# Expert layer on one core: the rows of each expert's list dealt round the partitions

## The reference, cut to what matters

```
g_sel = argmax(softmax(x @ w_rg)); top_p, top_i = top_k(softmax(le[g_sel]), 2)   # one of 4 groups, 2 of its 8 experts
gate  = p_sel * top_p / sum(top_p);  eid = g_sel * 8 + top_i
for each block of up to 128 rows of one expert e:
    y[rows] += gate * ((silu(x[rows] @ w_g[e]) * (x[rows] @ w_u[e])) @ w_d[e])
```

## Time and profile before

| what | value |
|---|---|
| median of 3 runs | 1541.19 us (1537.97 to 1541.45) |
| profiled execution | 1536.46 us, of which span 1535.0 us |
| TensorE busy | 1404.0 us, 91% of the span, mean granted clock 0.965 |
| VectorE, ScalarE, GpSimd busy | 1085.5, 859.4, 407.6 us |
| HBM read, written | 285.06 MB, 51.80 MB |
| weight loads | 96 x 2048 KB |
| gathers L2309, adding scatters L2318 | 32 and 30 |

### The profile page before, as it was taken

How to read it: one execution, slowest core, us unless ns; L and a number is a source line. 1 busy time by engine, 2 the same in 40 slices (tenths; PEclk the granted TensorE clock), 3 DMA queues, 4 the chain that set the end, 5 groups by cost and what they waited for, 6 DMA issues and landing times.

```text
span 1535.0 us, 23095 instructions
## 1 busy us (share of the span) xinstructions
PE 1404.0 (91%) x8472; PEld 1159.4 (76%) x8472; DVE 1085.5 (71%) x1526; ACT 859.4 (56%) x1029; POOL 407.6 (27%) x280
## 2 busy tenths in 40 slices
PE   5999899999978899986999959999999999999982
PEld 4788788888866777875888747888888777777771
DVE  4766765544456667663566768989998888888876
ACT  5644444433355555542444447777777777777764
POOL 2000111111132000000122243556654443444321
PEclk9999999999999999997999969999999999999996
DMA  8344412112311100013565558999999999999977
GB/s 272 118 152 145 161 66 103 68 65 83 103 42 49 58 25 28 15 49 116 171 247 211 197 196 305 390 392 393 387 392 385 378 367 375 370 379 381 380 270 292
DMA packets 63242, 329.12 MB, mean 214 GB/s; under 512 B 11862, under 2 KB 18406, under 8 KB 50882
## 3 DMA queue, kind: packets, MB, share of 16 engines
q1 hardware_dynamic: 45906, 278.60, 47.7%
q0 software_dynamic: 17264, 49.56, 10.6%
HBM read 285.06 MB, written 51.80 MB: 219 GB/s over the span
## 4 chain that ended last, share of the span: by engine, by line
PE 30%; DMA 13%; issue 4%; DVE 4%; ACT 2%; POOLq 0%; DVEq 0%; POOL 0%; SPq 0%; ACTq 0%
PE acc L96 9%; PE acc L98 9%; PE acc L97 9%; DMA plain<-in_w_gate 4%; DMA plain<-in_w_down 4%; DMA odd_gate<-in_w_gate 3%; ACT shared L1799 1%; PE acc L2414 1%; DVE even_lo L1804 1%; PE acc L2444 1%; PE acc L1994 1%; DVE plain L2617 1%; DMA s_x_mid<-plain 1%; DMA s_h_rows<-plain 1%; PE acc L2005 1%
## 5 line engine op out<-in xcount | busy, mean ns | idle before, releaser
L96 PE MATMUL acc<-shared,split 128*128 128x512 f32 x952 | 382.2, 401 | 16.8 <-DVE split L2062 11.4
L98 PE MATMUL acc<-shared,split 128*128 128x512 f32 x952 | 373.7, 393 | 0.0
L96 PEld LDWEIGHTS acc<-shared,split 128*128 128x128 f32 x952 | 180.9, 190 | 53.9 <-DVE split L2062 11.6
L1804 DVE TENSOR_TENSOR even_lo<-plain,shared 128x4096 fp32r<-128x4096 f32 x48 | 211.6, 4420 | 7.1 <-ACT shared L1799 6.3
L98 PEld LDWEIGHTS acc<-shared,split 128*128 128x128 f32 x952 | 180.3, 189 | 38.7
L96 PE MATMUL pa<-shared,a_xT_hi 128*128 128x512 f32 (+1 forms) x480 | 193.6, 403 | 16.2 <-DVE a_w_lo L736 14.0
L1799 ACT CAST shared<-plain 128x4096 fp32r<-128x4096 f32 x48 | 174.3, 3633 | 36.1 <-DMA plain<-in_w_up 14.5
L98 PE MATMUL pa<-shared,a_xT_lo 128*128 128x512 f32 (+1 forms) x480 | 187.0, 390 | 0.0
L97 PE MATMUL acc<-even_lo,split 128*128 128x512 f32 x384 | 150.6, 392 | 0.0
L1804 DVE TENSOR_TENSOR split<-odd_rest,shared 128x4096 fp32r<-128x4096 f32 x31 | 137.0, 4421 | 6.0 <-ACT shared L1799 5.8
L2309 POOL DMA_INDIRECT plain<-s_h_rows,plain x32 | 130.3, 4072 | 21.1 <-issue 11.8
(11 more groups left out here) (334 smaller groups left out, 2732.0 us busy)
## 6 DMA issues: line engine op xcount, KB each, us to landing
plain<-in_w_gate SPq DMA_DIRECT2D x16, 2048.0 KB, 19.6
plain<-in_w_up SPq DMA_DIRECT2D x16, 2048.0 KB, 20.4
plain<-in_w_down SPq DMA_DIRECT2D x16, 2048.0 KB, 20.3
odd_rest<-in_w_down SPq DMA_DIRECT2D x16, 2048.0 KB, 19.7
odd_gate<-in_w_gate SPq DMA_DIRECT2D x16, 2048.0 KB, 20.2
odd_rest<-in_w_up SPq DMA_DIRECT2D x16, 2048.0 KB, 21.3
a_x_turned<-in_x_turned SPq DMA_DIRECT2D x24, 512.0 KB, 3.5
a_x_row<-in_x SPq DMA_DIRECT2D x12, 512.0 KB, 4.9
```

Of the source, the lines that this page charges most:

```text
L96: pe.matmul(out, st_hi, mv_hi, start=first, stop=False)
L98: return pe.matmul(out, st_lo, mv_hi, start=False, stop=last)
L1804: eng.tensor_tensor(self.w_lo[half][m], self.raw[half][m][:, 0:4096], self.w_hi[m].bitcast(F32), ALU.subtract).then_inc(self.s_wlo[m], 1)
```

## The change

A helper `dealt` changes the order in which a table slice of 128 rows is read. The slice is seen as 8 groups of 16 rows and read with the 16 outermost: place 16h + l of a list goes to partition 8l + h, for h = 0 to 7 and l = 0 to 15. It is applied to each of the three fetches of lists. `places` gets the same order, so that the first expert's list, which does not come from the table, is dealt too. Rows, gates and table stay what they were; only the partition on which each row of a block stands is another, in the gather and in the adding scatter.

```diff
+ENGINES = 16
+
+def dealt(rows):
+    return rows.rearrange("(h l) c -> l h c", l=ENGINES)
...
-            nc.gpsimd.iota(places[:], pattern=[[1, P]], base=0, channel_multiplier=0,
+            nc.gpsimd.iota(places[:], pattern=[[1, ENGINES], [ENGINES, P // ENGINES]], base=0, channel_multiplier=0,
...
-                pool.dma_start(late[half][:], by_place[bass.ds(row, P), bass.ds(2 * e, 2)]).then_inc(s_late[half], 16)
+                pool.dma_start(late[half][:], dealt(by_place[bass.ds(row, P), bass.ds(2 * e, 2)])).then_inc(s_late[half], 16)
...
-            pool.dma_start(lists.rearrange("p e a -> p (e a)"), by_place[0:P, :]).then_inc(s_lists, 16)
+            pool.dma_start(lists.rearrange("p e a -> p (e a)"), dealt(by_place[0:P, :])).then_inc(s_lists, 16)
...
-                    pool.dma_start(late[0], by_place[0:P, 2 * NE - 4:2 * NE - 2]).then_inc(s_late[0], 16)
+                    pool.dma_start(late[0], dealt(by_place[0:P, 2 * NE - 4:2 * NE - 2])).then_inc(s_late[0], 16)
```

## The result

Over 20 runs each, the changed kernel takes 1543.57 us (median, 1540.18 to 1549.9) and the kernel before 1538.28 us (1535.66 to 1541.94). The ratio is 1.0038, with a 95% interval of 1.0028 to 1.0047: slower by 5.8 us by the ratio, where no change was forecast. The profiled execution has a span of 1541.9 us against 1535.0.

The account below looks back on a forecast made before the run. TensorE was taken to bound the expert stage's first half, the backlog of eight full DMA engines the second. Terms 0 + 0 + 0 on 1536.46 gave 1536.5 us, forecast as a median of 1541, 8 in 10 within 1533 to 1548.

Parts of the forecast that it names:

- What bounds the kernel: Expert stage: TensorE paces the first stretch at 17.79 us a block, weight transfers on eight full engines the second at 18.84.
- Partitions of an engine are not one run of eight; the deal leaves eight engines with eight rows: Gathers and adding scatters: an engine serves two runs of four partitions, so the deal only makes eight other engines full.
- The plateau near 0.5: Tail of the expert stage: DMA busy share near 0.5 for 5 us, read as eight of 16 engines still working.
- rival A: Expert stage: the deal evens the engines out, 18.0 us a block, some 15 us back, 1526 us; chance 0.09.
- After the change the full engines still have 16 rows a block: the term is 0: Expert stage blocks: row packets of each full engine stay at 16, so the deal itself changes the time by 0.
- Rival B: Expert stage: full engines get in each other's way, 0.4 us a block over 31 blocks, 12 us slower, 1553; chance 0.10.
- The argument against B and C: Expert stage: full engines keep the uncrowded price amid all traffic; in the tail all eight stop within one us after 1476.
- C: Expert stage: full engines disturb each other less or a slow one is relieved, 0.25 us a block gained, 1533; chance 0.07.
- The Trainium skill's sentence that DMA engines 7 and 15 are usually slower: Full engines: by this rule engine 7 loses its full share and C's time follows; the trace shows no such laggard.
- The fetch, the iota, the late fetches at 0: List fetches and iota: strided fetch +0 to +1 us, hidden; iota perhaps tenths, covered; late fetches 0; sum 0.
- The forecast of 1541 us: Whole kernel: profiled 1536.46 us plus zero terms gives 1536.5, taken as a median of 1541; no change, chance 0.74.
- the 4.6 us that were to tell a change from none: Whole kernel: faster or slower by 0.3%, or 4.6 us, is about what a measurement can tell.

Follow-up runs that it names:

- e4: Kernel before with lists dealt by the grouping in two runs of four partitions, so each engine gets 6 rows, once 5: ratio 0.9917 to the kernel before.
- e2: Kernel before with the two halves of each list exchanged, so the full engines are 8 to 15: ratio 1.0033 to the kernel before.
- e1: Kernel before with lists dealt only inside each half of the partitions, the same eight engines full: ratio 1.0016 to the kernel before.
- e11: e1 timed again, lists dealt inside each half of the partitions: ratio 1.0017 to the kernel before.
- e3: Kernel before with bits 6 and 4 of the place exchanged, full engines 0 to 3 and 8 to 11: ratio 0.9998 to the kernel before.
- e6: The changed kernel timed and profiled again: ratio 1.0036 to the kernel before.
- e10: Kernel before in its plain order, with lists fetched by two DMAs and an iota of two levels: ratio 0.9998 to the kernel before.
- e7: Kernel before with one extra 1 MB transfer on SyncE's queue at about block 2: ratio 1.0025 to the kernel before.
- e8: e4, the even deal, with the same extra 1 MB transfer at about block 2: ratio 0.9910 to the kernel before.
- e9: Kernel before with the halves of the lists exchanged for experts 16 to 31 only, two full sets in turn: ratio 0.9918 to the kernel before.
- e5: The kernel before itself, timed and profiled again as a control: ratio 1.0000.

## Why the prediction was wrong

- **What bounds the kernel**: right. The backlog of the full engines sets the pace of the second stretch; e4, which only spreads the rows, takes away every wait for weights.
- **Partitions of an engine are not one run of eight; the deal leaves eight engines with eight rows**: right. The plateau near 0.5 is there again, and rival A did not come.
- **"After the change the full engines still have 16 rows a block: the term is 0"**: this is the step that failed. The rows are the same, the term is not zero. It measured 5.8 us by the ratio; the profiles show 3.0 us up to the last turn, and some 4.6 up to the end of the kernel. The step took equal counts of rows for equal time. The runs show two things in its place: which engines are full matters (e2: 5.1 us for the same counts in the same order), and so does the order of the rows, for which the sum had no term at all (e1 and e11: some 2.6 us with the same engines full).
- **Rival B, priced at 12 us with a chance of 0.10**: the right sign, and right in that a full engine has no slack in which to make a delay good. Its price was too high: 3.0 / 31 = 0.1 us a block if the loss were spread evenly, where I took 0.4. But it is not spread evenly: 1.3 to 1.5 us stand after three blocks, where 0.1 a block would give 0.3 to 0.5. Its mechanism, neighbours, is not what the runs show: e2 keeps each set of neighbours as it was and costs 1.0033, and e3 makes full neighbours across the halves and costs nothing that can be measured.
- **The argument against B and C** is where the chance went wrong. I read in the tail of before that its eight full engines end together, and took that for a property of all sixteen. It says nothing of the other eight. In e2 and e6 the tail does fall in steps, with the last engines one to three microseconds behind.
- The Trainium skill's sentence that DMA engines 7 and 15 are usually slower ("DMA: Bandwidth & Descriptors", section "Latency and other measured facts") does not sort the sets: by its section on the swizzle, before holds 7, the change holds neither and is slower.
- **The fetch, the iota, the late fetches at 0**: right (e10, and 2.83 against 2.82 us from fetch to gather).
- **The forecast of 1541 us and its range** of 1533 to 1548 held the time, but by luck. The base was the median of three runs, 1541.19, where 20 runs give 1538.28: the forecast stood 2.9 us too high before any term, on the side on which the change then came out. The loss of 5.8 us is beyond the 4.6 us that were to tell a change from none.

What is shown: in this stage an early delay of the full engines costs time at the end, and of even ones it does not (e7 against e8); the cost depends on which engines are full (e2 against before, only the halves exchanged) and in part on the order (e1 against e10); spread in space (e4) or in time (e9), the same rows cost 12.8 and 12.6 us less. What is open: why some engines of the other sets come in later, where in the first three blocks the delay arises, and how an order whose neighbours are 16 places apart costs 2.6 us. One lead for the order, not shown: in the DMA packets of the traces (905 to 1500 us) a row of an adding scatter takes 327 ns (median) in every kernel, but its mean is 334 to 336 ns in before, e5, e7, e2 and e9, and 344 to 349 in all kernels that deal or exchange smaller pieces. Against it, e10 with the plain order has 343, and e3 has 349 and loses nothing. Of the 5.8 us some 1.2 are not seen behind the first turn; single profiles differ by as much.

## What to carry to other kernels

When rows are gathered by an index list with empty places at its end, count rows for each DMA engine over the whole stage, and not for one block: a transfer lands with its slowest engine, and an engine that is always full keeps a delay to the end. A deal has to follow the partitions that one engine serves, here two runs of four; dealt by neighbouring eights it only chooses another eight engines to be full. A busy share that stands at a simple fraction in a stretch without new loads tells how many engines are late, but not that they cost time: e9 shows such a share too and is as fast as the even deal. And two arrangements with the same count for each engine are not the same time until they are measured.

## What the runs showed of the hardware

- A 1 MB transfer at block 2, in a stretch where TensorE waited for nothing, cost 3.8 us (1.5 to 6.3) of the kernel's time, and nothing that could be measured once the rows were even.
- The same eight rows an engine cost 5.1 us more (1.0033, e2) on the upper 64 partitions than on the lower 64. I had expected the sixteen engines to be alike.
